# Second mixer: values as the stationary operand for two heads at a time, and the attention norm's factor applied in the output projection

## What is computed

```python
def neighbourhood_attention(q, k, v, rpb):          # 8 heads, 512 tokens
    ...
        s = s + bias.astype(F32)[None]
        p = jax.nn.softmax(s.reshape(B, NA_HEADS, GRID_W, kh * NA_KW), axis=-1)
        p = p.reshape(s.shape).astype(v_nb.dtype)
        return jnp.einsum('bhcij,bicjhd->bchd', p, v_nb)

def rms_norm_2(x, g):
    xf = x.astype(F32)
    y = xf * lax.rsqrt(jnp.mean(xf * xf, axis=-1, keepdims=True) + EPS)
    return (y * g.astype(F32)).astype(x.dtype)
```

## Time and profile before

| | us |
|---|---|
| median of 3 runs (2917.4 to 2921.08) | 2920.06 |
| the profiled execution | 2920.47 |
| its span, first to last instruction | 2918.6 |
| PE busy | 2663.2 |
| DVE busy | 1407.3 |
| ACT busy | 851.9 |
| second mixer, about | 1689 to 1864 |
| norm phase, about | 1864 to 1877 |
| output projection, about | 1877 to 1930 |
| router and experts | 1930 to 2919 |

### The profile page before, as it was taken

How to read it: one execution, slowest core, us unless ns; L and a number is a source line. 1 busy time by engine, 2 the same in 40 slices (tenths; PEclk the granted TensorE clock), 3 DMA queues, 4 the chain that set the end, 5 groups by cost and what they waited for, 6 DMA issues and landing times. The chain is left out here.

```text
span 2918.6 us, 34121 instructions
## 1 busy us (share of the span) xinstructions
PE 2663.2 (91%) x13117; PEld 1881.0 (64%) x13117; DVE 1407.3 (48%) x2367; ACT 851.9 (29%) x1419; POOL 694.5 (24%) x427
## 2 busy tenths in 40 slices
PE   7988889999999989999999899769988989989896
PEld 4846779999999978888887776544332333323332
DVE  4456449988778748888888344540000000010001
ACT  4244223336777733333333232410000000000001
POOL 0231016677888842222221020000000000000000
PEclk8989999999999989999999898789999999999999
DMA  7163215558999999999996231159999999999996
GB/s 290 40 240 138 87 59 177 172 187 282 367 379 384 370 363 349 363 357 363 353 361 241 79 115 43 62 207 393 427 428 428 428 427 428 428 427 428 427 428 269
DMA packets 211765, 860.52 MB, mean 295 GB/s; under 512 B 21063, under 2 KB 90695, under 8 KB 183736
## 3 DMA queue, kind: packets, MB, share of 16 engines
q1 hardware_dynamic: 156344, 699.44, 61.7%
q0 software_dynamic: 36864, 134.23, 11.9%
q10 hardware_dynamic: 18432, 25.17, 2.4%
HBM read 805.29 MB, written 53.49 MB: 294 GB/s over the span
## 5 line engine op out<-in xcount | busy, mean ns | idle before, releaser
L837 PE MATMUL val_banks<-val_v,val_coef_split 128*128 128x512 f32 x2268 | 516.9, 390 | 9.5 <-DVE val_coef_split L91 9.5
L837 PEld LDWEIGHTS val_banks<-val_v,val_coef_split 128*128 128x128 f32 x2268 | 427.5, 189 | 98.9 <-DVE val_v L91 9.8
L1098 PE MATMUL moe_up_ps<-all_raw_first,moe_xs_t 128*64 128x512 f32 x1632 | 435.2, 612 | 44.2 <-DMA all_raw_first<-in_up_tiles 34.0
L600 PE MATMUL dots_dot_ps<-both_acts,dots_u_split 128*128 128x384 f32 x2064 | 376.2, 339 | 17.2 <-POOL dots_u_split L91 17.2
L600 PEld LDWEIGHTS dots_dot_ps<-both_acts,dots_u_split 128*128 128x128 f32 x2064 | 361.1, 190 | 19.5 <-issue 10.0
L1098 PEld LDWEIGHTS moe_up_ps<-all_raw_first,moe_xs_t 128*64 128x64 f32 x1632 | 141.1, 140 | 288.4 <-issue 287.4
L91 POOL TENSOR_TENSOR dots_u_split<-dots_u_raw,dots_u_split 128x1024 fp32r<-128x1024 f32 x86 | 225.4, 2623 | 244.4 <-ACT dots_u_split L86 243.4
L1233 DVE TENSOR_TENSOR all_x<-moe_y_ps,all_x 128x512 f32<-128x512 f32 x64 | 44.1, 691 | 444.6 <-PE moe_y_ps L1066 444.5
L86 ACT CAST val_v<-both_shared 128x2048 fp32r<-128x2048 f32 x64 | 122.1, 1908 | 346.0 <-PE val_banks L837 346.0
L1304 POOL DMA_INDIRECT val_v_rows<-in_peer_v,one_expert x128 | 133.0, 1039 | 377.2 <-DVE val_banks L742 360.7
L1115 PE MATMUL moe_y_ps<-all_raw_first,moe_hid_t 128*64 128x512 f32 x768 | 195.7, 600 | 4.0 <-issue 2.7
(11 more groups left out here) (386 smaller groups left out, 3349.3 us busy)
## 6 DMA issues: line engine op xcount, KB each, us to landing
all_raw_first<-in_gate_tiles SPq DMA_DIRECT2D x51, 2048.0 KB, 30.7
all_raw_first<-in_up_tiles SPq DMA_DIRECT2D x51, 2048.0 KB, 31.0
all_raw_first<-in_w_down SPq DMA_DIRECT2D x48, 2048.0 KB, 33.0
both_shared<-in_peer_v SPq DMA_DIRECT2D x64, 1024.0 KB
dots_u_raw<-in_u_tiles SPq DMA_DIRECT2D x86, 512.0 KB
moe_raw_more<-in_w_down SPq DMA_DIRECT2D x16, 2048.0 KB, 32.5
moe_raw_more<-in_gate_tiles SPq DMA_DIRECT2D x13, 2048.0 KB, 29.7
moe_raw_more<-in_up_tiles SPq DMA_DIRECT2D x13, 2048.0 KB, 33.6
```

The costliest lines, as they stand in the source:

```text
L600: last = self.nc.tensor.matmul(self.banks[:, q % 2, 0:DENSE], self.split[q % 3][:, u_part, k], self.h_t[:, h_part, k, T - DENSE:T], start= ...
L837: last = nc.tensor.matmul(banks[:, 2 * (t + 1) + half, :], coef_split[:, b, c_part, a, t * P:(t + 1) * P], v[:, b, v_part, a, half * BANK: ...
L1098: last = nc.tensor.matmul(up_ps[of(e), b, :], xs_t[:, k, of(e)], w[e][:, b * BANK:(b + 1) * BANK], start=(k == 0), stop=(k == KD - 1))
```

## The change

Attention's products change sides. Values of two heads (each 128 x 64) are stationary, head a writes to partitions 64a to 64a+63 of one PSUM tile, and `expd_t` streams, 128 columns a product. A pair of units is done in every even step, the result has features on its partitions, and no transpose is needed after it. Since the softmax divisor now runs along the free axis, PE spreads the reciprocals with two products of the broadcast reciprocal against the identity, ACT copies them out (128x128), and DVE multiplies (128x128) in place of two scalings.

`norm_phase` is gone. Attention's gain and its high and low parts are made in the mixer (chunks 0 to 2 after steps 12, 20 and 28) and at the start of the new `second_out_phase` (chunk 3). There the attention's half of the projection has a PSUM sum of its own, and the factor 1/root mean square of each token is applied when that sum is added to `x`. The mean of squares comes from 16 products with a column of ones. Five of the eight weight pieces are asked for during the mixer.

```diff
+class TurnedAttention:
     # pe_step, even i >= 4, after the transposes of unit i-2
+            pe.wait_ge(self.inv_ready, 2 * pair + 2)
...
+            for a, u in enumerate(units):
+                last = nc.tensor.matmul(self.inv_ps[DH * a:DH * a + DH, place, :],
+                                        self.total_inv[:, u:u + 1].to_broadcast([P, DH]), self.ident[:],
+                                        start=True, stop=True)
+            last.then_inc(self.inv_spread, 1)
+            pe.wait_ge(self.turn_taken, 2 * pair + 2)
+            for c in range(NT):
+                for a, u in enumerate(units):
+                    last = nc.tensor.matmul(self.out_ps[DH * a:DH * a + DH, place, :], self.v_of(*self.units[u])[c],
+                                            self.expd_t[:, u % self.TURNS, c, :], start=(c == 0), stop=(c == NT - 1))
+            last.then_inc(self.weighed, 1)
     # act_step, between the copy of unit i-2 and the exponential of unit i
+            act.wait_ge(self.inv_spread, pair + 1)
...
+            nc.scalar.copy(self.inv_rows[:, pair % 2, :], self.inv_ps[:, pair % self.OUT, :]).then_inc(self.inv_taken, 1)
     # dve_step: the reciprocal of unit i-2, then for even i >= 4
+            dve.wait_ge(self.inv_taken, pair + 1)
+            dve.wait_ge(self.weighed, pair + 1)
+            nc.vector.tensor_tensor(self.o_of(*self.units[2 * pair]), self.out_ps[:, pair % self.OUT, :],
+                                    self.inv_rows[:, pair % 2, :], ALU.mult).then_inc(self.out_taken, 1)

 def second_mixer(...):
+    CHUNK_STEPS = (12, 20, 28)
                 # sync, after the last bias table
+                sp.wait_ge(side_done, G_BACK + 2)
+                for p in range(3):
+                    ahead.ask(sp, p)
+                sp.wait_ge(side_done, G_NORM + 1)
+                sp.wait_ge(y_ready, 2)
+                for p in range(3, AHEAD_OUT):          # AHEAD_OUT = 5
+                    ahead.ask(sp, p)
                 # scalar, in steps 12, 20, 28
+                        nc.scalar.activation(h_t[:, 0, 2 + c, :], attn[:, c, :], ACT.Copy,
+                                             scale=gain[:, 2 + c:3 + c]).then_inc(attn_hi, 1)
                 # vector, one step later
+                        dve.wait_ge(attn_hi, c + 1)
+                        nc.vector.scalar_tensor_tensor(out=h_t[:, 1, 2 + c, :], in0=attn[:, c, :],
+                                                       scalar=gain[:, 2 + c:3 + c], in1=h_t[:, 0, 2 + c, :].bitcast(F32),
+                                                       op0=ALU.mult, op1=ALU.subtract)

+def second_out_phase(nc, w_dram, attn, mix_t, gain, ones, x, ahead):
+    pieces = [(n, h) for n in range(2) for h in OUT_ORDER]      # OUT_ORDER = (0, 3, 1, 2)
             # tensor: 24 products a piece, and after piece 0
+                        pe.wait_ge(squared, NT)
+                        for t in range(NT):
+                            for c in range(NT):
+                                last = nc.tensor.matmul(sum_ps[:, t:t + 1], square[:, c, t * P:(t + 1) * P], ones[:, 0:1],
+                                                        start=(c == 0), stop=(c == NT - 1))
             # scalar
+                nc.scalar.activation(mix_t[:, 0, 2 + LAST, :], attn[:, LAST, :], ACT.Copy,
+                                     scale=gain[:, 2 + LAST:3 + LAST]).then_inc(attn_hi, 1)
+                hi(0)
+                for c in range(NT):
+                    nc.scalar.activation(square[:, c, :], attn[:, c, :], ACT.Square).then_inc(squared, 1)
+                for p in range(1, 4):
+                    hi(p)
+                act.wait_ge(mean_ready, 1)
+                nc.scalar.activation(root[:], mean[:], ACT.Sqrt).then_inc(root_ready, 1)
             # vector, when a sum is added to x
+                        if group == 0:
+                            ins = nc.vector.tensor_tensor(part, banks[:, 0, t, :], part, ALU.add)
+                        else:
+                            ins = nc.vector.scalar_tensor_tensor(out=part, in0=banks[:, 1, t, :], scalar=rstd[:, t:t + 1],
+                                                                 in1=part, op0=ALU.mult, op1=ALU.add)

-                norm_phase(nc, "an2", ident, attn, A["mix_norm_g_2"][0, HY:HY + NA], width=NA, to_t=acts, t_chunk0=2, ahead=ahead[3])
-                out_projection(nc, "out2", A["w_out_2"][0], acts, x, ahead[3])
+                second_out_phase(nc, A["w_out_2"][0], attn, acts, gain, ones, x, ahead[3])
```

More of the change, by code:

```diff
@@ L38 @@
 SPANS = DENSE // SPAN
+OUT_ORDER = (0, 3, 1, 2)
+AHEAD_OUT = 5
 NE = 16
@@ L226, with __init__ @@
     PLACES, TILES = 6, 2
-    def __init__(self, sem, room, w_dram, first_cols):
-        self.sem, self.w, self.first_cols = sem, weight_tiles(w_dram), first_cols
+    def __init__(self, sem, room, w_dram, first_cols, order=(0, 1, 2, 3)):
+        self.sem, self.w, self.first_cols, self.order = sem, weight_tiles(w_dram), first_cols, order
         self.raw = room[:, 0:self.PLACES * self.TILES * BANK].rearrange("p (b k n) -> p b k n", b=self.PLACES, k=self.TILES)
     def ask(self, sp, p):
-        n, h = p // (KD // self.TILES), p % (KD // self.TILES)
+        n, h = p // (KD // self.TILES), self.order[p % (KD // self.TILES)]
         sp.dma_start(self.raw[:, p], self.w[:, h * self.TILES:(h + 1) * self.TILES,
@@ L2215, in tables, with second_mixer @@
         return [self.head(h) for h in range(self.FIRST_TABLES)]
-def second_mixer(nc, A, ident, ones, h_t, qk, values, attn, hy_y, pool_y, spec_dram, gain, mix_loads, room):
+def second_mixer(nc, A, ident, ones, h_t, qk, values, attn, hy_y, pool_y, spec_dram, gain, mix_loads, room, ahead):
     PAD = 8
@@ L2344, in _ @@
                 step = Steps(pool, pool_step)
-                nc.gpsimd.memset(mat[:], 0.0).then_inc(zeroed, 1)
+                nc.gpsimd.memset(mat, 0.0).then_inc(zeroed, 1)
                 for c in range(2):
@@ L2453, in _ @@
                         nc.scalar.activation(norm_root[:], norm_root[:], ACT.Sqrt).then_inc(norm_root_ready, 1)
+                    if i in CHUNK_STEPS:
+                        c = CHUNK_STEPS.index(i)
+                        act.wait_ge(att.out_taken, NT * (c + 1))
+                        act.wait_ge(side_done, 8)
+                        act.wait_ge(gain_loaded, 16)
+                        nc.scalar.activation(h_t[:, 0, 2 + c, :], attn[:, c, :], ACT.Copy,
+                                             scale=gain[:, 2 + c:3 + c]).then_inc(attn_hi, 1)
                     if NORM_STEP + 4 <= i < NORM_STEP + 8:
@@ L2928, in program @@
             ahead = [Ahead(both.sem(f"ahead{i}"), shared, w, cols) for i, (w, cols) in enumerate((
-                (A["w_in"], (768, 1280)), (A["w_query"], (0, BANK)), (A["w_in_2"][0], (Q2, Q2 + BANK)),
-                (A["w_out_2"][0], (0, BANK))))]
+                (A["w_in"], (768, 1280)), (A["w_query"], (0, BANK)), (A["w_in_2"][0], (Q2, Q2 + BANK))))]
+            ahead.append(Ahead(both.sem("ahead3"), shared, A["w_out_2"][0], (0, BANK), OUT_ORDER))
             spec_stored = both.sem("spec_stored")
```

183 lines of the change are left out of this document (176 added, 7 removed).

## The result

The changed kernel takes **2904.43 us** (median of 5 runs, 2901.46 to 2908.21) against 2920.06 before (5 runs): ratio 0.9945, 95% interval 0.9932 to 0.9959, so 15.6 us faster. Forecast were 2911.9 and a range down to 2907.5: the sign was right, the size was not. A group is a set of kernels timed together on one chip, the kernel before always among them; the ratios are those on record and can differ in the last digit from the quotient of the medians.

What follows compares the result with a forecast made beforehand. The experts' weight stream starts when the projection ends, so gains before it move the end equally. Terms -12.2 + 3.4 + 0.2 - 1.1 + 2.0 - 0.5 - 0.4 + 0.4 = -8.2 give 2911.9 us; range 2907.5 to 2919.

Steps and rivals of the forecast that it cites:

- The norm phase and the loads, -12.2: Mixer's end to first projection product: 15.47 us shrinks to 3.24, if the five weight pieces are there; -12.2 us.
- +1.0 - 0.5: Mixer's end: step 30's pair at half clock costs +1.0 us; the last steps' products, started later but shorter, give -0.5.
- The sums, +3.4 and +0.2: Projection: 16 sums of squares between pieces 0 and 1 on PE, +3.4 us; last four additions becoming multiply-adds, +0.2.
- Rival C: Low clock in the sums of squares, which take 7.4 us, and piece 1 starting at half speed: +5, 2917; chance 0.11.
- Products where PE is the bound, -1.1: Steps 4 to 14, 20, 22, 26: a pair's products and spreading cost 1.49 against 1.62 us, -0.13 in nine pairs.
- The 0.3 for switching tile widths: Cost per pair of changing between 128-wide and 64-wide tiles on PE, 0.14 + 0.15 us.
- Products where a chain is the bound, +2.0: Late mixer steps, where DVE waits for both units' products: +0.5 us in step 24, +0.5 in 28, +1.0 in 30.
- Step 28: Mixer step where DVE's reciprocal, two multiplications and the next maximum queue behind the wait for products: +0.5 us.
- steps 9 to 11 at +0.4: Mixer steps where PE waits for ACT's and DVE's copies, which stand behind a new wait or copy: +0.4 us.
- steps 16 and 18 at -0.4: Mixer steps bound by DVE's spectrum work, which lose two scalings for one multiply, 0.2 us each: -0.4.
- Rival E: Less idle around 1864 brings full clock sooner and the mixer's low-clock stretches recover: -4, 2908; chance 0.06.
- Rival A: The halves don't run side by side at 128 columns, so a pair costs 2.7 us: +18, time 2930, slower; chance 0.10.

Runs made afterwards that it cites:

- four variants: Kernel after with one head's products before the other's; weight loads asked late; norm operations in odd steps; that plus later square root: 2913.99, 2913.29, 2902.21, 2899.26 us.
- like clock: Second trace of the unchanged kernel before, used as base for the mixer because the first had a low clock in step 20; 2919.90 us, ratio 0.9992.
- the one with the halves apart: Kernel after with all four products of the first head issued before the second's, instead of alternating; 2913.99 us, 0.9976 of the kernel before.

## Why the prediction was wrong

**The norm phase and the loads, -12.2: right.** 3.25 us from mixer to projection against 3.24, part by part, so not by luck, and the step 30 to projection stretch -11.7 as summed (-12.2 + 1.0 - 0.5). That both removals are needed was said as a condition ("only if the five weight pieces are there"); asking for the loads late took 6 to 8 of it away.

**The sums, +3.4 and +0.2: right in size, one effect missing.** 3.48 measured, and the last four additions took 2.73 where 2.48 stood, +0.25. Rival C had the low clock but on the wrong side: in the kernel after the clock was not low in the sums, it fell behind them, for +1.5 (only in four variants did it begin within them). The output phase grew by 4.8, not 3.6.

**Products where PE is the bound, -1.1: mis-sized.** -0.34 to -0.36 a pair in steps 4, 6 and 12, -0.30 in 14, 22 and 26. The products with the values and the spreading took 0.88 and 0.27 (forecast 0.95 and 0.24). The 0.3 for switching tile widths, read off rows with other shapes, was too high: 0.09 on each side. For the nine pairs it all comes to about -3 instead of -1.1.

**Products where a chain is the bound, +2.0: half right.** Step 24 +0.3 (forecast +0.5). From the scores of step 30 to the mixer's end 16.82 became 17.33, +0.5 as forecast (+1.0 - 0.5). Step 28 +1.7 (forecast +0.5). The prediction named what stands behind DVE's wait but not what stands ahead of ACT's copy for which it waits.

**The failed step: steps 9 to 11 at +0.4, steps 16 and 18 at -0.4.** Measured at like clock -4.3 (steps 8 to 12, products included) and -2.9. The working counted in those steps what DVE and ACT do more or less, and the new waits. That is the part of the path that it had wrong: it did not ask what the *removed* wait had held: L1693 of an odd step stood ahead of DVE's side work and made it wait 3 to 4 us for products that PE issued last. Reordering DVE in the kernel before gave -3.7 and -2.9 in the same steps.

**The mixer summed up**, step 2 to 30 at like clock: -1.9 (six pairs), -0.9 (step 2, which the prediction left out: the first unit's products wait for step 4), -4.3 (steps 8 to 12), -2.9 (16 to 20), +1.3 (20, clock), +0.3 (24), +1.7 (28), together -6.8 where -0.1 was forecast.

**The base.** The first trace's steps 20 to 22 had 3.8 us of low clock that its second trace doesn't have; the kernel after has 1.3 each time. Rival E, "more than forecast through the clock", named the direction and not the cause: most of it was DVE's order. At like clock the stretch changed by -13.6, and from its first trace by -17.8; the measured 15.6 lie between.

**Slips in the working.** Rival A's +18 doesn't follow from its own terms: 14 x 1.2 and two pairs at 2.4 give 21.6. Step 30's +1.0 is 2.45 - 1.6 = 0.85, and nine pairs at 0.13 are 1.2. None of them bears on what failed.

## What to carry to other kernels

When a change removes a wait, list what was queued behind it on that engine as carefully as for a wait that it adds, above all where the engine serves two streams: putting side work ahead of a wait on a late product gave the kernel before 9 us (5 to 12) by itself. Two latencies side by side are worth little singly, here 0.5 and 3.7 of 12 us, so price them together. And take the base of a ledger from two traces: one step pair here differed by 3.8 us between executions of the same kernel.

## What the hardware showed

- Products of 64 stationary columns and 128 streamed go side by side, two records in 0.109 us, when the queue alternates halves; 16 records take 0.97. With one half's records first they take 1.46, and the first and last four start singly, 0.109 apart. The switch from 128-wide tiles costs 0.09, and so does the return.
- 32 records of one streamed column, 0.109 us each, keep PE busy in the profile and at full clock, and the granted clock behind them, in the stretch shown, is 0.54 (0.50 to 0.56 in nine traces). Eight of them do not do this (1.00 in four traces).
- With the new mixer steps 20 to 22 ran at a granted clock of 0.86 (11.96 to 11.98 us) in ten traces, and at 1.00 (10.87) in the one with the halves apart. With waits put back on DVE that stretch steps 16 to 18 from 4.03 to 6.09, they ran at 1.00 (10.39) in two traces, and the low clock lay in steps 18 to 20 (0.52 and 0.71). In the kernel before they took 10.69, 10.68 and 14.48, and with DVE reordered 12.29 and 13.98: there nothing can be told from single traces.
